# Four weight slots outside the ring, refilled through the whole expert loop: even experts read their first half there, odd experts in the ring

## The chip, the core and the metric

The kernel runs on one core of a Trainium2 chip, in float32. Its time is the device time of one execution in microseconds (us); the time of a version is the median of several executions. A profile is taken of one further execution. The engines are PE (TensorE), DVE (VectorE), ACT (ScalarE), POOL (GpSimd) and SP (SyncE), which here does nothing but issue transfers; 16 DMA engines move the data.

## The reference

One decoder layer for 256 prompt tokens and 8 sample tokens: a mixer (an RG-LRU group beside a convolution group), cross-attention, and then 32 routed experts of which each token takes four. The change lies in the experts:

```python
def run_block(args):
    e, idx = args
    xb = x_pad[idx]
    gu = xb @ w_e1[e] + b_e1[e]
    g, u = gu[:, :D_EXPERT], gu[:, D_EXPERT:]
    g = jnp.minimum(g, SWIGLU_LIMIT)
    u = jnp.clip(u, -SWIGLU_LIMIT, SWIGLU_LIMIT)
    h = (u + 1.0) * (g * jax.nn.sigmoid(SWIGLU_ALPHA * g))
    return h @ w_e2[e] + b_e2[e]
```

`w_e1[e]` is 1024 x 2048 and `w_e2[e]` 1024 x 1024, so an expert has 12 MB of weights (1 MB = 1024 KB here), and all 32 are read once.

## The kernel before

**Slots.** On chip, weights stand in slots of 128 partitions x 2048 floats, 1 MB each. `ring` has `RING` = 12 of them. In the expert loop slots 0 to 7 hold `w_e1` of an expert (the eight blocks of its contraction) and slots 8 to 11 hold `w_e2`. They are filled two at a time, 2 MB in one transfer, into the even slot and the next. Four more slots, called `head`, lie outside the ring in memory that the attention no longer needs (`mn`, `kT`, `wgate` with a piece of `mix`, and `xT`). They are filled once, ahead of the loop, with the first half of expert 0; the ring then holds the rest of expert 0 and, in its slots 0 to 3, already the first half of expert 1.

**What PE does for an expert.** `up_bias(b)` waits for the bias row (`b1_filled`) and opens the sums with it (L1453); it reads `b1q`, the one buffer for a bias. `up` then takes slots 0 to 7 in order (L1539) and frees each with an increment of `freed`. ACT and DVE make the activation out of the sums (L1103, L686, L1106, L1109), PE turns it (`turn_h`, L1548), and `down` takes slots 8 to 11 (L1558), each again freed. Experts go in pairs `q`. In the even expert 2q, PE adds up the pair before (`rounds`, L1501) between `up` and `down`. In the odd expert, PE gathers the next pair's tokens (L1510) after slot 3 and after slot 7. Expert 0 is an exception: its bias is already in, and it takes a ring slot and a head slot in turn.

**What SP does.** SP issues all the weight transfers in the order of its program, each after a wait on `freed` for the slots that it writes. All of its transfers go through one hardware queue, q1. `expert(e, b)` issues six loads of 2 MB; the load for slots s and s + 1 waits until the expert before has used slot s + 1. The bias of expert e is a transfer of 8 KB, four rows of 2 KB, and it is issued before expert e's six loads, as soon as PE has used the bias of e - 1:

```python
with sp.Fori(2, NE) as e:
    sp.wait_ge(S["b1_used"], e)
    bias(e)
    expert(e, e)
```

Below, "load e:s" is the load of slots s and s + 1 for expert e; it fetches 2 MB. The last loads of the kernel are 31:0, 31:2, ..., 31:10. After the loop come the last rounds (L1501, L1617), the final norm on DVE (L1138, L1169) and the stores.

Of the kernel before, what the change touches and what calls it, by code (L numbers as in the profile page):

```python
# [76 lines left out]
HEAD_SLOTS = W_SLOTS // 2  # L77
KC_SLOTS = 8
# [28 lines left out]
def fills_before(n):  # L107

    return n // RING + 1 - (1 if n % RING < HEADROOM else 0)


def build(nc, a, outs):
    ctx = ExitStack()
    with ctx:
# [10 lines left out]
        EXPERT_W = ATTENTION_W + D  # L125
        MIXW = max(MIXER_W, EXPERT_W)
        mix = sb("mix", [P, MIXW])
        xT = sb("xT", [P, KD, TOK])
# [4 lines left out]
        mn = sb("mn", [P, KD, NMEM])  # L133
        kT = sb("kT", [P, KD, NMEM])
        wgate = sb("wgate", [P, 2, LC, P])
# [60 lines left out]
        head_u = mix[:, ATTENTION_W:EXPERT_W]  # L196
# [7 lines left out]
        def table(*shape):  # L204
# [17 lines left out]
        head = [v[:, 0:SLOT].rearrange("p (g c) -> p g c", g=2) for v in  # L222
                (mn[:, :, :].rearrange("p k m -> p (k m)"), kT[:, :, :].rearrange("p k m -> p (k m)"),
                 xT[:, :, :].rearrange("p k t -> p (k t)"))]
        head = [(v[:, 0, :], v[:, 1, :]) for v in head]
        head.insert(2, (wgate[:, :, :, :].rearrange("p g c i -> p (g c i)"), head_u))
# [40 lines left out]
        head_filled consts zeroed ident_ready pick_ready freed kc_freed  # L267
# [45 lines left out]
        def _(sp):  # L313
# [50 lines left out]
            def fill_head(k):  # L364
                for gu in range(2):
                    sp.dma_start(head[k][gu], a["w_e1"][0, 0, DEAL[k], D * gu:D * gu + D]).then_inc(S["head_filled"], 16)


            sp.wait_ge(S["freed"], freed_after(KV_ENTRY[7]))
            fill_head(0)  # L370
            sp.wait_ge(S["score_done"], H)
            fill_head(1)
            fill_head(2)
# [8 lines left out]
            fill_head(3)  # L382
# [13 lines left out]
            with sp.If(n > 0):  # L396
                sp.wait_ge(S["table_ready"], 1)
                with sp.Fori(0, n) as j:
                    e = sp.value_load(tabi[0:1, 0, bass.ds(j, 1)], min_val=0, max_val=NE - 1)
                    sp.wait_ge(S["b1_used"], j + NE)  # L400
                    bias(e)
                    expert(e, j + NE)
# [771 lines left out]
        def _(pe):  # L1174
# [346 lines left out]
            def up(b, e2, between, outside=False):  # L1521

                if not outside:
                    up_bias(b)
                order = list(range(W_SLOTS))
                if outside:
                    order = [k for i in range(HEAD_SLOTS) for k in (HEAD_SLOTS + i, i)]
                for n_done, k in enumerate(order):
                    g_u = (ring[:, k, 0:D], ring[:, k, D:2 * D])
                    if outside and k < HEAD_SLOTS:  # L1530
                        pe.wait_ge(S["head_filled"], 2 * 16 * HEAD_SLOTS)
                        g_u = head[k]
                    elif k < HEAD_SLOTS:
                        pe.wait_ge(filled[k - k % 2], 16 * b + 16 * (fills_before(MOE0 + k) - 1))
                    else:
                        pe.wait_ge(filled[k - k % 2], 16 * b + 16 * fills_before(MOE0 + k))
                    for gu in range(2):
                        for i in range(2):
                            m = pe.matmul(ps[gu][CAP * i:CAP * i + CAP, :], xeT[:, k, CAP * e2:CAP * e2 + CAP],  # L1539
                                          g_u[gu][:, 512 * i:512 * i + 512],  # L1540
                                          start=False, stop=(n_done == W_SLOTS - 1))
                    m.then_inc(S["freed"], 1)
                    between(k)
# [20 lines left out]
            def pair(q, first):  # L1564
# [10 lines left out]
                if first:  # L1575
                    up(2 * q, 0, lambda k: None, True)
                    turn_h(2 * q)
                else:
                    up(2 * q, 0, lambda k: None)
# [6 lines left out]
                up(2 * q + 1, 1, gather_next)  # L1586
# [34 lines left out]
            with pe.If(n > 0):  # L1621
# [7 lines left out]
                with pe.Fori(0, n) as j:  # L1629
# [4 lines left out]
                    up(j + NE, 0, lambda k: None)  # L1634
# [34 lines left out]
```

## Time and profile before

| what | value |
|---|---|
| median of 3 executions | 1260.92 us (1260.77 to 1263.11) |
| the profiled execution's own time | 1263.79 us |
| its span, first to last instruction | 1261.4 us |
| PE busy | 1163.7 us (92%) |
| DMA queue q1, share of 16 engines | 87.5% |
| read from HBM | 453.71 MB |
| granted TensorE clock, mean | 0.980 of 2.4 GHz |

The profile cuts the span in 40 slices of 31.5 us. The expert loop lies between 312 us and 1247 us, slices 10 to 39. Matmuls overlap, so a busy PE is not one that could do no more; where PE waits for a transfer, the timeline has the wait in brackets behind the instruction that waited.

### The profile page before, as it was taken

What the parts mean: (1) busy time and instruction counts of PE and PEld (TensorE: products, weight loads), DVE (VectorE), ACT (ScalarE), POOL (GpSimd) and SP (SyncE); (2) the same over time, 40 slices, a digit from 0 to 9 for tenths busy, and PEclk for the clock granted to TensorE, in tenths of its full rate; (3) what the DMA queues carried; (4) which work ended last, traced back from release to release, by engine and by line L of the source; (5) the groups of instructions that cost most, each with busy time, mean ns of one, the idle gap of its engine ahead of it and who ended that gap; (6) DMA issues with size and microseconds to landing.
All of it is one profiled execution on the core that took longest, in us unless ns stands there. A gap on an engine that the chain in (4) does not pass through costs nothing.

```text
span 1261.4 us, 14407 instructions
## 1 busy us (share of the span) xinstructions
PE 1163.7 (92%) x5540; PEld 572.1 (45%) x5540; DVE 338.5 (27%) x820; ACT 182.1 (14%) x354; POOL 27.8 (2%) x54
## 2 busy tenths in 40 slices
PE   8999999698899999999998998989998989898996
PEld 6887888387333433434333333334333323232332
DVE  3795424515112121220212121212112021212123
ACT  3114213103010101011110101011110101010102
POOL 4000001100000000000000000000000000000000
PEclk9999999798889999999999999999999999999999
DMA  9398433993689999999999999999999999999993
GB/s 304 91 291 275 137 102 134 357 410 122 241 351 418 428 428 428 427 429 428 426 430 426 429 428 428 428 427 429 427 430 426 429 428 428 427 430 426 430 427 143
DMA packets 65381, 457.38 MB, mean 363 GB/s; under 512 B 4788, under 2 KB 33676, under 8 KB 41030
## 3 DMA queue, kind: packets, MB, share of 16 engines
q1 hardware_dynamic: 63408, 452.26, 87.5%
q10 hardware_dynamic: 1117, 3.04, 0.6%
q0 software_dynamic: 832, 1.76, 0.5%
q8 instruction: 16, 0.26, 0.1%
q14 instruction: 8, 0.06, 0.0%
HBM read 453.71 MB, written 3.81 MB: 363 GB/s over the span
## 4 chain that ended last, share of the span: by engine, by line
PE 56%; DMA 37%; DVE 4%; ACT 2%; issue 1%; ACTq 0%; POOL 0%; SPq 0%; DVEq 0%
DMA ring<-in_w_e 36%; PE ps L1539 21%; PE ps L1250 11%; PE ps L1558 8%; PE ps L1269 3%; PE ps L1501 3%; DVE ring L955 2%; PE ps L1510 2%; PE ps L1453 1%; PE ps L1412 1%; PE ps L1548 1%; PE ps L1499 1%; PE ps L1197 1%; PE ps L1186 1%; PE ps L1444 1%
## 5 line engine op out<-in xcount | busy, mean ns | idle before, releaser
L1539 PE MATMUL ps<-ring,mix 128*64 128x512 f32 x2016 | 452.2, 597 | 27.1 <-DMA ring<-in_w_e 25.0
L1539 PEld LDWEIGHTS ps<-ring,mix 128*64 128x64 f32 x2016 | 137.1, 137 | 326.6 <-issue 257.1
L1558 PE MATMUL ps<-ring,mix 128*64 128x512 f32 x1024 | 232.7, 607 | 22.0 <-issue 11.0
L1103 DVE TENSOR_SCALAR mix<-ps 128x512 f32<-128x512 f32 x32 | 22.1, 692 | 601.4 <-PE ps L1539 601.4
L1558 PEld LDWEIGHTS ps<-ring,mix 128*64 128x64 f32 x1024 | 78.7, 139 | 155.4 <-issue 141.2
L686 ACT ACTIVATE mix<-mix 128x512 f32<-128x512 f32 x32 | 20.2, 630 | 415.8 <-DVE mix L1103 415.8
L1510 PEld LDWEIGHTS ps<-mix 128*128 128x128 f32 x544 | 68.0, 200 | 14.4 <-issue 13.0
L1510 PE MATMUL ps<-mix 128*128 128x128 f32 x544 | 72.6, 288 | 1.3 <-ACT rstd L668 1.3
L696 ACT ACTIVATE mix<-ps 64x512 f32<-64x512 f32 x64 | 37.9, 592 | 226.5 <-PE ps L1558 226.1
L1090 DVE SCALAR_TENSOR_TENSOR mix<-mix,gates 128x1024 f32<-128x1024 f32 x16 | 20.5, 1284 | 151.5 <-ACT mix L696 151.5
L1501 PE MATMUL ps<-mix 128*128 128x512 f32 x128 | 59.2, 605 | 1.3 <-ACT mix L696 1.3
L1250 PE MATMUL ps<-mix,ring 128*128 128x264 f32 x256 | 58.8, 393 | 0.3 <-ACT mix L639 0.3
L1269 PE MATMUL ps<-ring,mn 128*128 128x256 f32 x256 | 56.1, 379 | 0.0
L1250 PEld LDWEIGHTS ps<-mix,ring 128*128 128x128 f32 x256 | 49.5, 194 | 9.1 <-ACT mix L639 0.4
L1269 PEld LDWEIGHTS ps<-ring,mn 128*128 128x128 f32 x256 | 48.6, 190 | 6.6
L1084 DVE TENSOR_TENSOR tok<-tok,ps 128x512 f32<-128x512 f32 (+1 forms) x70 | 43.5, 681 | 15.3 <-PE ps L1499 14.1
L841 DVE SCALAR_TENSOR_TENSOR mix<-mix,par 128x256 f32<-128x256 f32 x120 | 47.6, 491 | 0.0
L1250 PE MATMUL ps<-sq,ring 128*128 128x264 f32 x192 | 44.6, 396 | 0.0
L1250 PEld LDWEIGHTS ps<-sq,ring 128*128 128x128 f32 x192 | 37.4, 196 | 6.6
L1501 PEld LDWEIGHTS ps<-mix 128*128 128x128 f32 x128 | 23.0, 189 | 37.3 <-issue 35.1
L1250 PE MATMUL ps<-xn,ring 128*128 128x264 f32 x176 | 39.6, 387 | 0.0
L1548 PE MATMUL ps<-ident,mix 128*128 128x128 f32 x128 | 22.6, 300 | 15.4 <-DVE mix L1109 15.4
(294 smaller groups left out, 657.7 us busy)
## 6 DMA issues: line engine op xcount, KB each, us to landing
ring<-in_w_e SPq DMA_DIRECT2D x190, 2048.0 KB, 23.7
ring<-in_w_in SPq DMA_DIRECT2D x8, 1024.0 KB, 15.2
ring<-in_cache_mem_k SPq DMA_DIRECT2D x8, 1024.0 KB, 4.9
ring<-in_cache_mem_v SPq DMA_DIRECT2D x8, 1024.0 KB, 8.4
ring<-in_w_k SPq DMA_DIRECT2D x4, 1024.0 KB, 8.9
ring<-in_w_v SPq DMA_DIRECT2D x4, 1024.0 KB, 12.5
ring<-in_w_out SPq DMA_DIRECT2D x4, 1024.0 KB, 12.4
ring<-in_w_q SPq DMA_DIRECT2D x4, 1024.0 KB, 12.0
```

The source lines that it names most:

```text
L696: m = act.activation(ysb[CAP * e2:CAP * e2 + CAP, 512 * i:512 * i + 512], ps[3][CAP * i:CAP * i + CAP, :], ACT.Copy)
L841: dve.scalar_tensor_tensor(out=gc[:, c, 0:SEQ], in0=gpad[:, c, bass.ds(w, SEQ)], scalar=par[:, bass.ds(4 * w + (C_WCF + c), 1)], in1=gc[:, ...
L955: last = dve.tensor_tensor_reduce(key[:, t, h, :], key[:, t, h, :], q, 1.0, 0.0, ALU.mult, ALU.add, sT[:, t, 4 * b + h:4 * b + h + 1])
L1084: last = dve.tensor_tensor(dst, dst, ps[bank + i][0:rows, :], ALU.add)
L1103: dve.tensor_scalar(g1, ps[0][:, :], LIMIT, None, ALU.min).then_inc(S["g_clamped"], 1)
L1250: m = pe.matmul(ps[o % 4][:, 0:TOK], wslot(n)[:, k, half * P:(half + 1) * P], (xn if o < 4 else sq)[:, k, :] if kind == "in" else src(k), ...
L1269: m = pe.matmul(ps[KV_BANK[j]][:, 256 * t:256 * t + 256], mn[:, k, P * t:P * t + P], wslot(n)[:, k, :], start=(k == 0), stop=(k == KD - 1))
L1501: m = pe.matmul(ps[bank + i][:, :], gT[:, t0:t0 + P], ysb[:, cols], start=True, stop=True)
L1510: m = pe.matmul(ps[4 + i][:, P * (k % 4):P * (k % 4) + P], xnt[:, t, DEAL[k]], sel[:, t, :], start=(t == 0), stop=(t == 1))
L1539: m = pe.matmul(ps[gu][CAP * i:CAP * i + CAP, :], xeT[:, k, CAP * e2:CAP * e2 + CAP], g_u[gu][:, 512 * i:512 * i + 512], start=False, stop ...
L1548: m = pe.transpose(ps[2][:, j * P:(j + 1) * P], hh[:, j:4 * P:4], ident[:, :])
L1558: m = pe.matmul(ps[3][CAP * i:CAP * i + CAP, :], hTv[:, k % 4, CAP * (k // 4):CAP * (k // 4) + CAP], ring[:, s, D * (k % 2) + 512 * i:D * ...
```

## The change

Each head slot is from now on refilled during the loop. The two tensors `mixed` and `low` replace `mn`, `kT`, `mix`, `wgate` and `xT`, so that each pair of head slots is one piece of memory: `low` for slots 0 and 1, `high` (the end of `mixed`) for slots 2 and 3. A pair of them takes one transfer of 2 MB, with its own semaphore.

- Even experts read slots 0 to 3 from `low` and `high`; odd experts read them from the ring. So load e:0 or e:2 goes where expert e - 2 read its own. Slots 4 to 11 stay as they were.
- Ahead of the loop the same half of expert 0 is fetched; of slots 2 and 3 the part `LATE` = 1984 of 4096 columns comes early and the rest where `head[3]` came.
- Expert 0 takes its slots in the order 4, 5, 0, 1, 6, 7, 2, 3. During it, SP issues 1:4, 2:0, 1:6, 2:2, then 1:8 and 1:10.
- SP's loop is over pairs. The bias of expert e is issued behind load e:4.

```diff
+FIRST_ORDER = [4, 5, 0, 1, 6, 7, 2, 3]
...
-            def expert(e, b, first=0):
-
-                for s in range(first, RING, 2):
-                    fill(e, s, RING * b + freed_after(MOE0 + s + 1 - RING))
+            def refill(e, s, free):
+
+                sp.wait_ge(S["freed"], free)
+                sp.dma_start((low[:, :], high)[s // 2], first_weight(e, s)).then_inc(S[("low_filled", "high_filled")[s // 2]], 16)
+
+            def used(b, s):
+
+                return RING * b + freed_after(MOE0 + s)
+
+            def rest(e, b):
+
+                fill(e, 4, used(b - 1, 5))
+                sp.wait_ge(S["b1_used"], b)
+                bias(e)
+                fill(e, 6, used(b - 1, 7))
+                fill(e, 8, used(b - 1, 9))
+                fill(e, 10, used(b - 1, 11))
...
+            fill(1, 4, used(0, FIRST_ORDER.index(5)))
             sp.wait_ge(S["b1_used"], 1)
             bias(1)
-
-            for s in range(HEAD_SLOTS, W_SLOTS, 2):
-                fill(1, s, freed_after(MOE0 + 2 * (s + 1 - HEAD_SLOTS)))
-            expert(1, 1, W_SLOTS)
-            with sp.Fori(2, NE) as e:
-                sp.wait_ge(S["b1_used"], e)
-                bias(e)
-                expert(e, e)
+            refill(2, 0, used(0, FIRST_ORDER.index(1)))
+            fill(1, 6, used(0, FIRST_ORDER.index(7)))
+            refill(2, 2, used(0, FIRST_ORDER.index(3)))
+            fill(1, 8, used(0, 9))
+            fill(1, 10, used(0, 11))
+
+            def two_experts(q, last):
+
+                for s in range(0, HEAD_SLOTS, 2):
+                    fill(2 * q + 1, s, used(2 * q - 1, s + 1))
+                rest(2 * q, 2 * q)
+                if not last:
+                    for s in range(0, HEAD_SLOTS, 2):
+                        refill(2 * q + 2, s, used(2 * q, s + 1))
+                rest(2 * q + 1, 2 * q + 1)
+
+            with sp.Fori(1, PAIRS - 1) as q:
+                two_experts(q, False)
+            two_experts(PAIRS - 1, True)
...
-            def up(b, e2, between, outside=False):
+            def up(b, q, e2, between, even=False, outside=False):
...
-                for n_done, k in enumerate(order):
-                    g_u = (ring[:, k, 0:D], ring[:, k, D:2 * D])
-                    if outside and k < HEAD_SLOTS:
-                        pe.wait_ge(S["head_filled"], 2 * 16 * HEAD_SLOTS)
-                        g_u = head[k]
-                    elif k < HEAD_SLOTS:
-                        pe.wait_ge(filled[k - k % 2], 16 * b + 16 * (fills_before(MOE0 + k) - 1))
+                for n_done, k in enumerate(FIRST_ORDER if outside else range(W_SLOTS)):
+                    w = ring[:, k, :]
+                    if k >= HEAD_SLOTS:
+                        pe.wait_ge(filled[k - k % 2], 16 * b + 16 * fills_before(MOE0 + k))
+                    elif not even:
+                        pe.wait_ge(filled[k - k % 2], 16 * q + 16 * fills_before(MOE0 + k))
                     else:
-                        pe.wait_ge(filled[k - k % 2], 16 * b + 16 * fills_before(MOE0 + k))
+                        w = head[k]
+                        pe.wait_ge(S[("low_filled", "high_filled")[k // 2]], 16 * q + 32)
```

The first place is SP's loop. Before, one turn of it is one expert e: the bias first (`in_b_e1`), then the six loads, four from `w_e1` and two from `w_e2`. These are the turn's first rows, as far as its third load:

```order
L361 ISA [waits b1_used]
L361 DMA mix<-in_b_e1 4x512
L345 ISA
L353 ISA [waits freed]
L353 DMA ring<-in_w_e1 128x4096
L345 REGISTER_ALU
L353 ISA [waits freed]
L353 DMA ring<-in_w_e1 128x4096
L345 REGISTER_ALU
L353 ISA [waits freed]
L353 DMA ring<-in_w_e1 128x4096
```

After the change one turn is a pair. Its first two loads are (2q+1):0 and (2q+1):2, the next is 2q:4, and only then comes the bias of 2q:

```order
L356 ISA [waits freed]
L356 DMA ring<-in_w_e1 128x4096
L348 REGISTER_ALU
L356 ISA [waits freed]
L356 DMA ring<-in_w_e1 128x4096
L348 REGISTER_ALU
L356 ISA [waits freed]
L356 DMA ring<-in_w_e1 128x4096
L377 ISA [waits b1_used]
L377 DMA mixed<-in_b_e1 4x512
L348 REGISTER_ALU
L356 ISA [waits freed]
```

So the bias has moved from ahead of an expert's first load to behind the third load of the same stretch. In the middle of the turn the same piece comes again for the odd expert, with `low` and `mixed` as the targets of the two loads ahead:

```order
L361 ISA [waits freed]
L361 DMA low<-in_w_e1 128x4096
L360 REGISTER_ALU
L361 ISA [waits freed]
L361 DMA mixed<-in_w_e1 128x4096
L348 REGISTER_ALU
L356 ISA [waits freed]
L356 DMA ring<-in_w_e1 128x4096
L377 ISA [waits b1_used]
L377 DMA mixed<-in_b_e1 4x512
```

The second place is expert 0's stretch of SP's program, just ahead of the loop. Before, it is the bias of expert 1 and loads 1:4, 1:6, 1:8, 1:10:

```order
L361 DMA mix<-in_b_e1 4x512
L353 DMA ring<-in_w_e1 128x4096 x2
L353 DMA ring<-in_w_e2 128x4096 x2
```

After, it has two loads more, 2:0 into `low` and 2:2 into `mixed`:

```order
L356 DMA ring<-in_w_e1 128x4096 [waits freed]
L377 DMA mixed<-in_b_e1 4x512 [waits b1_used]
L361 DMA low<-in_w_e1 128x4096 [waits freed]
L356 DMA ring<-in_w_e1 128x4096 [waits freed]
L361 DMA mixed<-in_w_e1 128x4096 [waits freed]
L356 DMA ring<-in_w_e2 128x4096 [waits freed] x2
```

## Rows read from the trace of the kernel before

**Rows 1.** The page's 40 slices: PE, granted clock, DMA share and rate.

```profile
PE   8999999698899999999998998989998989898996
...
PEclk9999999798889999999999999999999999999999
DMA  9398433993689999999999999999999999999993
GB/s 304 91 291 275 137 102 134 357 410 122 241 351 418 428 428 428 427 429 428 426 430 426 429 428 428 428 427 429 427 430 426 429 428 428 427 430 426 430 427 143
```

**Rows 2.** Stretches of the loop: busy us of each engine, PEclk, DMA share, GB/s.

```profile
312.00:318.00 6.00, 5.79 (x28) 2.46 (x30) 0.00 (x0) 0.11 (x1) 0.00 (x0) 1.00 0.00 0
318.00:338.00 20.00, 16.32 (x65) 5.83 (x62) 4.22 (x12) 1.23 (x2) 0.00 (x0) 0.83 0.58 211
338.00:368.00 30.00, 29.30 (x136) 12.07 (x132) 4.98 (x8) 3.67 (x7) 0.00 (x0) 0.92 1.01 418
368.00:373.00 5.00, 5.00 (x20) 1.46 (x20) 0.26 (x1) 0.00 (x0) 0.00 (x0) 0.78 0.04 16
...
388.00:1240.00 852.00, 792.32 (x3790) 304.41 (x3787) 157.23 (x314) 89.36 (x162) 0.00 (x0) 1.00 1.00 427
```

**Rows 3.** The chain that ended last, expert 3 and experts 29 to 31: start, us, what.

```profile
405.21 7.02 PE ps L1539 x32
...
1147.03 25.66 DMA ring<-in_w_e
...
1172.74 3.68 PE ps L1539 x16
1176.43 0.04 SPq L353
...
1176.57 25.64 DMA ring<-in_w_e
...
1206.08 25.66 DMA ring<-in_w_e
1231.75 0.04 issue
1231.79 3.68 PE ps L1539 x16
```

**Rows 4.** PE's timeline, experts 30 and 31: start, us, instructions [wait before them].

```profile
1187.80 1.09 PE L1453 MATMUL ps<-mix,ones 1*64 1x512 f32 x8
1188.82 7.31 PE L1539 MATMUL ps<-ring,mix 128*64 128x512 f32 x32
1197.37 3.65 PE L1539 MATMUL ps<-ring,mix 128*64 128x512 f32 x16 [1.24 <-DMA ring<-in_w_e]
1202.25 3.65 PE L1539 MATMUL ps<-ring,mix 128*64 128x512 f32 x16 [1.23 <-DMA ring<-in_w_e]
...
1217.71 1.09 PE L1453 MATMUL ps<-mix,ones 1*64 1x512 f32 x8
1218.73 7.09 PE L1539 MATMUL ps<-ring,mix 128*64 128x512 f32 x32
...
1228.00 7.45 PE L1539 MATMUL ps<-ring,mix 128*64 128x512 f32 x32
```

**Rows 5.** PE's timeline: the start of expert 0, and the pair of experts 2 and 3.

```profile
312.21 1.94 PE L1539 MATMUL ps<-ring,mix 128*64 128x512 f32 x8 [1.11 <-issue]
...
377.35 1.09 PE L1453 MATMUL ps<-mix,ones 1*64 1x512 f32 x8
378.37 13.95 PE L1539 MATMUL ps<-ring,mix 128*64 128x512 f32 x64
...
404.13 1.09 PE L1453 MATMUL ps<-mix,ones 1*64 1x512 f32 x8
...
432.91 1.09 PE L1453 MATMUL ps<-mix,ones 1*64 1x512 f32 x8
```

**Rows 6.** SP's timeline: the issue of expert 31's bias.

```profile
1189.10 0.56 SPq L361 DMA_DIRECT2D mix<-in_b_e  x1
```

**Rows 7.** Two places where the granted clock fell in the loop: PE's timeline.

```profile
329.16 1.13 PE L1548 MATMUL ps<-ident,mix 128*128 128x128 f32 x4 [3.00 <-DVE mix L1109]
330.98 9.62 PE L1558 MATMUL ps<-ring,mix 128*64 128x512 f32 x32 [0.69 <-ACT mix L690]
...
885.49 8.78 PE L1558 MATMUL ps<-ring,mix 128*64 128x512 f32 x32 [0.73 <-issue]
...
1239.84 7.09 PE L1558 MATMUL ps<-ring,mix 128*64 128x512 f32 x32 [0.73 <-issue]
```

**Rows 8.** Stretches of 2 us in which the clock was at its lower level.

```profile
332.00:334.00 2.00, 2.00 (x8) 0.59 (x6) 0.00 (x0) 0.00 (x0) 0.00 (x0) 0.50 0.00 0
336.00:338.00 2.00, 2.00 (x12) 0.70 (x10) 0.00 (x0) 0.00 (x0) 0.00 (x0) 0.97 0.00 0
```

More of the change, by code:

```diff
@@ L124, in build @@
         ATTENTION_W = 2 * KD * TOK + 2 * H * 2 * NMEM + 2 * D + 4 * NB * H + 2 * P
[L125 to L128, printed above, removed]
+        MIXW = max(MIXER_W, ATTENTION_W)
+        LATE = 2 * SLOT - KD * TOK
+        low = sb("low", [P, 2 * SLOT])
+        mixed = sb("mixed", [P, MIXW + 2 * LC * P + KD * TOK])
+        mix = mixed[:, 0:MIXW]
+        wgate = mixed[:, MIXW:MIXW + 2 * LC * P].rearrange("p (g c i) -> p g c i", g=2, c=LC)
+        xT = mixed[:, MIXW + 2 * LC * P:MIXW + 2 * LC * P + KD * TOK].rearrange("p (k t) -> p k t", k=KD)
+        high = mixed[:, MIXW + 2 * LC * P + KD * TOK - 2 * SLOT:MIXW + 2 * LC * P + KD * TOK]
+        mn = low[:, 0:SLOT].rearrange("p (k m) -> p k m", k=KD)
+        kT = low[:, SLOT:2 * SLOT].rearrange("p (k m) -> p k m", k=KD)
         xn = sb("xn", [P, KD, TOK])
@@ L219, in build @@
         gateT = rstd[0:NE, :]
[L222 to L226, printed above, removed]
+        assert MIXW + 2 * LC * P + KD * TOK - 2 * SLOT >= ATTENTION_W
+        head = [v[:, SLOT * i:SLOT * i + SLOT] for v in (low, high) for i in range(2)]
         tabi = sb("tabi", [1, 2, P], I32)
@@ L341, in _, with first_weight @@
                             sp.dma_start(stage_b[r0:r0 + rows, :], src).then_inc(S["par_loaded"], 16)
+            def first_weight(e, s):
+                return a["w_e1"][0][bass.ds(e, 1), s * P:(s + 2) * P, :].rearrange("o (p t) c -> p (o t c)", t=2)
             def fill(e, s, free):
@@ L362, in bias @@
                     S["b1_filled"], 16)
-            def fill_head(k):
-                for gu in range(2):
-                    sp.dma_start(head[k][gu], a["w_e1"][0, 0, DEAL[k], D * gu:D * gu + D]).then_inc(S["head_filled"], 16)
             sp.wait_ge(S["freed"], freed_after(KV_ENTRY[7]))
-            fill_head(0)
+            sp.dma_start(low[:, 0:SLOT], a["w_e1"][0, 0, DEAL[0], :]).then_inc(S["low_filled"], 16)
             sp.wait_ge(S["score_done"], H)
-            fill_head(1)
-            fill_head(2)
+            sp.dma_start(low[:, SLOT:2 * SLOT], a["w_e1"][0, 0, DEAL[1], :]).then_inc(S["low_filled"], 16)
+            sp.dma_start(high[:, 0:LATE], first_weight(0, 2)[:, 0:LATE]).then_inc(S["high_filled"], 16)
             for s in range(HEAD_SLOTS, W_SLOTS, 2):
@@ L399, in _ @@
                     e = sp.value_load(tabi[0:1, 0, bass.ds(j, 1)], min_val=0, max_val=NE - 1)
-                    sp.wait_ge(S["b1_used"], j + NE)
-                    bias(e)
-                    expert(e, j + NE)
+                    for s in range(0, HEAD_SLOTS, 2):
+                        fill(e, s, used(j + NE - 1, s + 1))
+                    rest(e, j + NE)
             for t in range(2):
@@ L1575, in pair @@
                 if first:
[L1576 removed]
+                    up(2 * q, q, 0, lambda k: None, True, True)
                     turn_h(2 * q)
                 else:
[L1579 removed]
+                    up(2 * q, q, 0, lambda k: None, True)
                     pe.wait_ge(S["y_ready"], 2 * q)
@@ L1585, in pair @@
                 down(2 * q)
-                up(2 * q + 1, 1, gather_next)
+                up(2 * q + 1, q, 1, gather_next)
                 gather(q + 1, (1,))
```

17 lines of the change are left out of this document (5 added, 12 removed).

## The prediction

> **What bounds the kernel now.** I read the 40 slices first. From the fourteenth slice to the last but one the DMA row is full, at 426 to 430 GB/s [rows 1], and the stretch 388 to 1240 us taken as one has a share of 1.00 at 427 GB/s [rows 2]. Ahead of it the DMA engines have holes: nothing moves from 312 to 318 us, 211 GB/s from 318 to 338, and 16 GB/s from 368 to 373 [rows 2]. Those holes are SP waiting for a free slot.
>
> The chain says the same in another way. Near the end it is one load of 25.65 us, two slots of matmuls of 3.68 us, the next load [rows 3]. PE takes up the load's slots at 1172.74, then 29.5 us later, and last at 1231.79. In 29.5 us six loads of 2 MB land, so one takes 4.92 us. A load that lands 25.65 us after its issue has thus four others before it in the queue: slots come free long before they can be refilled, and the rate of the DMA engines sets the pace, not the number of slots.
>
> How far behind is PE? Early, with no wait, an even expert takes 404.13 - 377.35 = 26.78 us and an odd one 432.91 - 404.13 = 28.78 us [rows 5]. The loads allow 29.5 us each. So PE has 2.7 us to spare in an even expert and 0.7 us in an odd one.
>
> **What the change removes and adds. First term, the slots.** Holes can be filled only where a slot comes free earlier than before. That is so once: in expert 0, where the head slots used to lie idle after use. Two more loads, 2:0 and 2:2, are issued there, 2 x 4.92 = 9.8 us of transfer. From 318 to 338 us, 20 us at 211 GB/s moved 4.2 million bytes, which are two loads; four take 19.7 us. Expert 0 begins at 312.21, and two slots of matmuls take 3.5 us (eight take 13.95) [rows 5], so the first load can go out at 315.7 and the four are through by about 336, before the slots of `down` come free at 338. The hole holds them, and nothing behind is late.
>
> From then on, count the loads by the event that releases them. Before, the use of slot s + 1 of expert e - 1 releases load e:s, for all six s. After, for s of 4 and more it releases the same load e:s; for s of 0 and 2 it releases (e+1):s. At each event 2 MB, in both versions. So the queue is as long as before at each moment, the hole at 368 to 373 us stays, and **loads e:4 to e:10 land when they landed before**. Only the loads for slots 0 to 3 land earlier, by a whole expert. Were they late? PE sat at slots 4 and 6 of expert 30, 1.24 and 1.23 us, and its matmuls of slots 0 to 3 took 7.31 us where those of expert 31 took 7.09, 0.2 us [rows 4]; and that 0.2 is only taken out of the next wait. The lead of two loads is held as four full slots in memory and never spent, except in the last pair: there is no load 32:0 or 32:2, so 31:4 to 31:10 land 9.8 us earlier. But expert 31 had waited only 7.45 - 7.09 = 0.36 us for them [rows 4]; the rest of the 9.8 finds PE behind. First term: -0.4 us at the most.
>
> **Second term, the bias.** `up_bias` stands at the head of an expert, ahead of slots 0 to 3. Before, the bias of 31 is issued at 1189.10 and needed at 1217.71 [rows 4, 6]; it lies in the queue ahead of load 31:0. After, it lies behind 31:4, three loads later, and of expert 30 behind 30:4. When does that land? PE's slot 4 of expert 30 ended its wait at 1197.37 [rows 4], and by the count above 30:4 lands at that time again. The 8 KB behind it add about 0.1. So **expert 30 can't begin before 1197.5**, where it began at 1187.80 [rows 4]: 9.7 us late.
>
> What is given back? The waits of expert 30. Four slots take 7.02 us with no wait [rows 3], two 3.51. Slot 4 would have begun without a wait at 1188.82 + 7.02 = 1195.84 and did at 1197.37: 1.53. Slot 6 at 1197.37 + 3.51 = 1200.88 and did at 1202.25: 1.37. Both are gone, since their loads have landed by then: 2.9 us. In expert 31 the 0.36 goes as well, which is the first term. Expert 31 itself doesn't wait for its bias: 31:4 now lands four loads after 30:4, at 1197.4 + 19.7 = 1217.1, and PE comes at 1197.5 + 26.9 = 1224.4. What follows, to the end of the kernel, hangs on PE. The sum is 9.7 - 2.9 - 0.4 = **+6.4 us**. By the durations of an unhindered expert it is 1197.5 + 26.8 - 1217.71 - 0.36 = +6.2. I take +6.3.
>
> Does the DMA pace hold when PE is late? Slot 7 comes free 9.7 - 2.9 = 6.8 us later. The load then has 25.65 - 6.8 = 18.9 us from issue to landing, of which it needs 4.9 itself: three loads are still queued. So the loop keeps its 29.5 us per expert; what is lost is lost once, as a later place of PE against the loads, and only the end of the kernel pays it. PE's waits change their place: at the head of an odd expert 29.5 - 26.8 = 2.7 us, at the head of an even one 29.5 - 28.8 = 0.7 us. They begin some experts earlier than the first waits of before.
>
> **Third term, code and memory.** PE runs the same matmuls on the same shapes; a pair has one register instruction less or more here and there, which I take as 0. Ahead of the loop the same bytes are loaded. The load of slots 2 and 3 is split otherwise, 64 columns of 128 rows later: 32 KB, under 0.1 us, and expert 0 comes to slot 2 at about 322 us.
>
> **The time.** The sum is made against the profiled execution: 1263.79 + 6.3 = 1270.1. That one stands 2.9 us above the median of the runs, so the median becomes 1260.92 + 6.3 = 1267.2.
>
> **The rivals.**
>
> *The lead arrives (faster).* If the two loads of lead moved every landing, the loop would end 9.8 us earlier: 1251.1. For it speaks that the DMA row is the full one. Against it speaks the count: each load that PE waits for has two more ahead of it in the queue, the two of the lead. It would decide if PE had waited for slots 0 to 3, and those waits are 0.2 us. "Perfetto Trace Analysis", section Optimization Strategy, of the Trainium skill says that consistent bubbles can mean too little SBUF for the next tile; by that rule four more slots would close the 1.24 us bubbles here. The trace speaks against it, since the DMA share in the same stretch is 1.00. Chance 0.05.
>
> *The bias doesn't gate (no change).* If 8 KB passed the 2 MB loads, only -0.4 is left: 1260.5. Against it: the same queue, and loads that land 25.65 us after issue. Chance 0.04.
>
> *The bias lands early.* It has four rows, a load 128, so it need not use all DMA engines. If those that it uses run ahead of the others by up to a load, it lands up to 4.9 us earlier, expert 30 begins at 1192.6, and its slot 4 at 1200.6, still behind the load's 1197.4. Then the loss is 6.3 - 4.9 = 1.4 at the least: 1262.3 to 1266. "DMA: Bandwidth & Descriptors", section Queues, rings and completion order, says that descriptors are taken in ring order on each engine, but that completion isn't first in, first out over DMAs spread over different numbers of engines. No row here shows how far the engines lie apart. Chance 0.08.
>
> *The clock.* After a PE wait of 3.00 us the granted clock was 0.50, the 1.2 GHz level [rows 7, 8], and `down` took 9.62 us where it takes 7.09; a second fall, at 885 us, cost 8.78 - 7.09 = 1.7 [rows 7]. The new wait of 2.7 us at the head of each odd expert comes near that first one. The spare 3.4 us of a pair swallows it, except what is left at the head of expert 30: after a fall in expert 29 it begins 1.7 - 0.7 = 1.0 to 2.9 - 0.7 = 2.2 us later. Then 1268.2 to 1269.4. Chance 0.18.
>
> *Later still.* If the bias were done only with the load behind it, 4.9 more: 1272. Chance 0.04.
>
> The forecast itself has 0.61; its own range, from the two ways to work out the sum and the half us of a fall that is partly swallowed, is 1266 to 1268.
>
> **How the numbers follow.** A change within 0.2% is 2.5 us, about what a measurement of this kernel can tell from none: 1258.4 to 1263.4. The forecast, the clock and the later bias are slower, as is half or more of the early bias: 0.61 + 0.18 + 0.04 + 0.05 = 0.88. Within: 0.03 + 0.04 = 0.07. Faster: 0.05. The range 1264 to 1271 holds the forecast, the clock and part of the early bias, 0.61 + 0.18 + 0.04 = 0.83.
>
> **What would show it.** In the new profile: between 318 and 338 us over 400 GB/s; 368 to 373 us still empty; the share 1.00 after it. PE's waits for loads at the `up` matmuls nearly gone, and in their place waits ahead of the bias matmuls, some 2.7 and 0.7 us in turn. Expert 30's bias matmuls near 1197.5. The last load landing near 1232 instead of 1231.75 + 2 x 4.92 = 1241.6, with PE 6 us later than before. The prediction is wrong if the bias matmuls don't wait, if slots 4 and 6 still do, or if the landing of 30:4 has moved.

## The result, and the profile after

The changed kernel takes 1270.69 us, the median of five executions (1268.37 to 1273.34), beside 1260.94 us before (five executions, 1260.77 to 1263.42). The ratio is 1.0068, with a 95% interval of 1.0048 to 1.0088: slower, by 6 to 11 us. A later measurement of the same kernel gave 1.0047 (1.0035 to 1.0059). The profiled execution took 1270.69 us with a span of 1268.4; that of before 1263.79 with 1261.4. So the two traces differ by 6.9 us, where the medians differ by 9.75. The time ahead of the loop is part of that; it is taken up below, under "Where an execution starts its loop".

The page's 40 slices of the changed kernel, the lines that answer to [rows 1]:

```profile
PEclk9989999898889999999999999999999999999999
DMA  9398323993989999999999999999999999999970
GB/s 302 90 295 269 137 100 133 354 407 129 398 351 415 428 429 428 428 429 427 429 428 427 430 426 428 430 427 428 428 429 429 427 429 427 429 429 426 429 309 35
```

The eleventh slice went from 241 to 398 GB/s: the hole of expert 0 is filled. The last two slices went from 427 and 143 to 309 and 35: the loads are over earlier. The same in chosen stretches, the lines that answer to [rows 2], and behind them three from the end of the loop (clock, DMA share and GB/s are the last three figures):

```profile
312.00:318.00 6.00, 6.00 (x30) 2.42 (x28) 0.00 (x0) 0.00 (x0) 0.00 (x0) 1.00 0.31 66
318.00:338.00 20.00, 16.31 (x64) 5.81 (x62) 4.22 (x12) 1.23 (x2) 0.00 (x0) 0.83 1.00 412
338.00:368.00 30.00, 29.30 (x134) 11.88 (x130) 5.24 (x8) 3.67 (x7) 0.00 (x0) 0.92 0.97 412
368.00:373.00 5.00, 5.00 (x22) 1.62 (x20) 0.00 (x0) 0.00 (x0) 0.00 (x0) 0.81 0.16 36
...
1206.00:1232.00 26.00, 25.31 (x114) 8.71 (x112) 6.61 (x16) 2.41 (x4) 0.00 (x0) 1.00 0.86 341
...
1208.00:1210.00 2.00, 2.00 (x12) 0.60 (x10) 0.00 (x0) 0.00 (x0) 0.00 (x0) 1.00 0.31 131
...
1232.00:1242.00 10.00, 10.00 (x56) 4.49 (x52) 0.00 (x0) 0.38 (x1) 0.00 (x0) 1.00 0.12 49
```

The last of these stretches in the kernel before:

```profile
1232.00:1242.00 10.00, 8.44 (x46) 4.30 (x44) 2.67 (x4) 2.10 (x4) 0.00 (x0) 1.00 0.59 252
```

The two extra loads fit into 318 to 338 us, and the hole at 368 to 373 us is still there. In stretches of 2 us the last weights arrive by 1234 us, before the change by about 1240: some 6 us sooner, not the 9.8 us of two loads. The DMA engines have gaps in the last pair (a share of 0.31 from 1208 to 1210 us), where no load 32:0 or 32:2 stands in the queue and PE is late to free the slots. The kernel still ends 7 us later. What does PE wait for? First the view of PE's waits before (us in total, times, longest), then after:

```profile
PE ps L1539 <- DMA ring<-in_w_e: 25.0, 21, 1.3
```

```profile
PE ps L1478 <- DMA mixed<-in_b_e: 27.2, 17, 2.7
```

The 21 waits for weights are gone. In their place PE waits 17 times ahead of L1478, the bias matmuls, for the transfer of 8 KB, up to 2.7 us. PE's timeline of the changed kernel from expert 28's `down` to expert 31's first half, to be laid beside [rows 4]:

```profile
1159.09 7.09 PE L1580 MATMUL ps<-ring,mixed 128*64 128x512 f32 x32 [0.69 <-ACT mixed L715]
1167.80 1.26 PE L1478 MATMUL ps<-mixed,ones 1*64 1x512 f32 x8 [1.62 <-DMA mixed<-in_b_e]
1168.99 8.56 PE L1561 MATMUL ps<-ring,mixed 128*64 128x512 f32 x32
...
1198.23 1.09 PE L1478 MATMUL ps<-mixed,ones 1*64 1x512 f32 x8
1199.25 3.65 PE L1561 MATMUL ps<-low,mixed 128*64 128x512 f32 x16
1202.73 3.60 PE L1561 MATMUL ps<-mixed 128*64 128x512 f32 x16
1206.16 7.04 PE L1561 MATMUL ps<-ring,mixed 128*64 128x512 f32 x32
...
1225.00 1.09 PE L1478 MATMUL ps<-mixed,ones 1*64 1x512 f32 x8
```

Expert 30 begins at 1198.23, where it began at 1187.80: 10.4 us late. Its slots 0 to 7 go through without a wait, which gives back 3.1 us, and expert 31 begins at 1225.00 where it began at 1217.71: 7.3 us late. From there to the end it is 43.4 us (43.7 before). Expert 29 shows a cost that the sum didn't have: its matmuls of slots 0 to 3 took 8.56 us instead of 7.09, behind a wait of 1.62 us. The clock had fallen, as the stretches there show (the third figure from the right is the granted clock):

```profile
1168.00:1170.00 2.00, 2.00 (x12) 0.40 (x7) 0.00 (x0) 0.00 (x0) 0.00 (x0) 0.65 0.94 401
1170.00:1172.00 2.00, 2.00 (x8) 0.61 (x6) 0.00 (x0) 0.00 (x0) 0.00 (x0) 0.50 1.02 434
```

In stretches of 2 us from 372 to 1240 us, the changed kernel has eight such falls, the kernel before one (at 885 us, [rows 7]). Only the one in expert 29 can reach the end: the earlier ones are followed by further waits for a bias, which take them up.

The chain that ended last has changed in kind. Before, a load was its link of 25.65 us [rows 3]; after, it is the bias:

```profile
1080.43 10.48 PE ps L1561 x48
...
1090.92 0.04 SPq L356
...
1091.57 17.24 DMA mixed<-in_b_e
...
1108.86 1.09 PE ps L1478 x8
```

Slots 4 and 5 are used, SP issues the load for them and the bias behind it, and the next expert begins when that bias lands.

**Where an execution starts its loop.** Executions differ ahead of the loop, whatever the kernel. In the eleven profiles of this document expert 2 begins near 374 us (373.94 to 374.23, four of them) or between 375.96 and 377.82 us (the other seven, the kernel before and both profiles of the changed kernel among them). The difference is the granted clock in experts 0 and 1. PE's timeline of the changed kernel, and then of a kernel of the other kind (`a5` below), with `down` of expert 0 and the start of expert 2; in between, in expert 1, one group of L1524 takes 3.60 us in the first and 1.98 in the second:

```profile
330.47 9.68 PE L1580 MATMUL ps<-ring,mixed 128*64 128x512 f32 x32 [0.69 <-ACT mixed L715]
...
376.91 1.09 PE L1478 MATMUL ps<-mixed,ones 1*64 1x512 f32 x8
```

```profile
330.38 8.46 PE L1580 MATMUL ps<-ring,mixed 128*64 128x512 f32 x32 [0.69 <-ACT mixed L715]
...
373.94 1.09 PE L1478 MATMUL ps<-mixed,ones 1*64 1x512 f32 x8
```

So traces are best compared from the start of expert 2 to the end of the span. In the kernel before that is 1261.4 - 377.35 = 884.1 us; the others are given against it:

| profile | expert 2 begins | end of span | from there to the end | against before | forecast, without falls |
|---|---|---|---|---|---|
| changed kernel | 376.91 | 1268.4 | 891.5 | +7.4 | +6.3 |
| changed kernel, second profile (c1) | 377.82 | 1271.2 | 893.4 | +9.3 | +6.3 |
| bias first (a1) | 374.05 | 1257.5 | 883.5 | -0.6 | -0.4 |
| bias one load earlier (a2) | 376.47 | 1261.7 | 885.2 | +1.2 | +1.3 |
| bias one load later (a3) | 377.62 | 1298.4 | 920.8 | +36.7 | +11.2 |
| before, bias late (b1) | 374.23 | 1267.6 | 893.4 | +9.3 | +8.9 |
| matmuls in the wait (a4) | 376.10 | 1268.3 | 892.2 | +8.2 | +6.3 |
| the same, not in the last pair (a5) | 373.94 | 1264.7 | 890.8 | +6.7 | +6 |
| rotating slots (s1) | 375.96 | 1249.9 | 873.9 | -10.1 | -9.8 |
| rotating, one bias buffer (s2) | 373.94 | 1253.4 | 879.5 | -4.6 | -5.7 |

### The profile page after: what moved, and what is told of

Same layout as the page of the kernel before. It is cut to its first block, busy times and chain, and to the rows that moved or that the text cites. A ratio compares the mean times of both kernels' runs of the same rounds, so it can differ in the third digit from the quotient of the medians.

```text
span 1268.4 us, 14301 instructions
## 1 busy us (share of the span) xinstructions
PE 1169.2 (92%) x5540; PEld 579.3 (46%) x5540; DVE 338.4 (27%) x820; ACT 182.1 (14%) x354; POOL 28.3 (2%) x54
## 4 chain that ended last, share of the span: by engine, by line
PE 68%; DMA 22%; DVE 5%; ACT 2%; issue 1%; SPq 1%; ACTq 0%; POOL 0%; DVEq 0%
PE ps L1561 32%; DMA mixed<-in_b_e 22%; PE ps L1275 11%; PE ps L1580 9%; PE ps L1294 3%; PE ps L1535 3%; PE ps L1478 3%; DVE ring L980 2%; PE ps L1526 1%; PE ps L1570 1%; DVE mixed L1131 1%; DVE mixed L1128 1%; DVE mixed L1134 1%; PE ps L1524 1%; PE ps L1222 1%
## 5 line engine op out<-in xcount | busy, mean ns | idle before, releaser
L1561 PE MATMUL ps<-ring,mixed 128*64 128x512 f32 x1536 | 354.0, 615 | 1.1 <-issue 1.1
L1580 PE MATMUL ps<-ring,mixed 128*64 128x512 f32 x1024 | 231.1, 604 | 22.0 <-issue 11.0
L1561 PEld LDWEIGHTS ps<-ring,mixed 128*64 128x64 f32 x1536 | 111.0, 141 | 228.1 <-issue 226.2
L1580 PEld LDWEIGHTS ps<-ring,mixed 128*64 128x64 f32 x1024 | 78.2, 139 | 154.3 <-issue 140.1
L1535 PEld LDWEIGHTS ps<-mixed 128*128 128x128 f32 x544 | 68.1, 200 | 14.4 <-issue 13.0
L1535 PE MATMUL ps<-mixed 128*128 128x128 f32 x544 | 72.7, 288 | 1.3 <-ACT rstd L693 1.3
L1478 PE MATMUL ps<-mixed,ones 1*64 1x512 f32 x256 | 35.5, 624 | 27.2 <-DMA mixed<-in_b_e 27.2
L1526 PE MATMUL ps<-mixed 128*128 128x512 f32 x128 | 59.2, 605 | 1.3 <-ACT mixed L721 1.3
L1275 PE MATMUL ps<-mixed,ring 128*128 128x264 f32 x256 | 58.9, 393 | 0.3 <-ACT mixed L664 0.3
L1561 PE MATMUL ps<-low,mixed 128*64 128x512 f32 x256 | 58.4, 598 | 0.0
L1561 PE MATMUL ps<-mixed 128*64 128x512 f32 x256 | 57.7, 592 | 0.0
L1294 PE MATMUL ps<-ring,low 128*128 128x256 f32 x256 | 56.1, 379 | 0.0
L1275 PEld LDWEIGHTS ps<-mixed,ring 128*128 128x128 f32 x256 | 49.6, 194 | 9.1 <-ACT mixed L664 0.4
## 6 DMA issues: line engine op xcount, KB each, us to landing
ring<-in_w_v SPq DMA_DIRECT2D x4, 1024.0 KB, 11.2
```

Of the source, the lines that this page charges most:

```text
L1275: m = pe.matmul(ps[o % 4][:, 0:TOK], wslot(n)[:, k, half * P:(half + 1) * P], (xn if o < 4 else sq)[:, k, :] if kind == "in" else src(k), ...
L1294: m = pe.matmul(ps[KV_BANK[j]][:, 256 * t:256 * t + 256], mn[:, k, P * t:P * t + P], wslot(n)[:, k, :], start=(k == 0), stop=(k == KD - 1))
L1478: m = pe.matmul(ps[gu][CAP * i:CAP * i + CAP, :], ones[r:r + 1, 0:CAP], b1q[r:r + 1, :], start=True, stop=False)
L1526: m = pe.matmul(ps[bank + i][:, :], gT[:, t0:t0 + P], ysb[:, cols], start=True, stop=True)
L1535: m = pe.matmul(ps[4 + i][:, P * (k % 4):P * (k % 4) + P], xnt[:, t, DEAL[k]], sel[:, t, :], start=(t == 0), stop=(t == 1))
L1580: m = pe.matmul(ps[3][CAP * i:CAP * i + CAP, :], hTv[:, k % 4, CAP * (k // 4):CAP * (k // 4) + CAP], ring[:, s, D * (k % 2) + 512 * i:D * ...
```

## Experiments

My theory, Q: the whole loss is the bias's place in the queue, since an expert can't begin before its bias, and the bias now lies behind a load that is needed later than it. The rivals: S, the refilled slots cost by themselves; L, the lead of two loads is worth something once the bias is out of the way; C, beside Q, falls of the clock add to it. Each kernel was timed against the kernel before on the same chip.

### The bias issued first again

```diff
             def two_experts(q, last):
 
+                next_bias(2 * q, 2 * q)
                 for s in range(0, HEAD_SLOTS, 2):
                     fill(2 * q + 1, s, used(2 * q - 1, s + 1))
                 rest(2 * q, 2 * q)
+                next_bias(2 * q + 1, 2 * q + 1)
...
-                sp.wait_ge(S["b1_used"], b)
-                bias(e)
```

> The changed kernel, with the bias of each expert issued where the kernel before issues it: ahead of the six loads of its stretch, so ahead of loads (e+1):0, (e+1):2 and e:4. Theory Q (the bias's place in the queue is the whole loss): the bias lands 14.7 us earlier, no expert waits for it, and only the last pair's 0.4 us is left of the change: 1260.5 us, and the granted clock in the loop as before. Rival S (the refilled slots themselves cost, or PE reads them more slowly): it stays at 1268 to 1271. Rival L (the lead of two loads is worth something once the bias is out of the way): up to 9.8 us under before, 1251.

Measured: 1260.97 us (11 executions), ratio 0.9996 (0.9986 to 1.0006). The loss is gone, nothing is gained, and the profile has no fall of the clock in the loop. Rival S falls with it, for this kernel refills the same slots by the same loads. Rival L falls too in this form: the lead is there, the stretch 318 to 338 us ran at 417 GB/s, and it brings nothing. PE waits for weights as before, at slots 4 and 6 of expert 30 (PE's timeline):

```profile
1193.80 3.65 PE L1567 MATMUL ps<-ring,mixed 128*64 128x512 f32 x16 [1.41 <-DMA ring<-in_w_e]
1198.69 3.65 PE L1567 MATMUL ps<-ring,mixed 128*64 128x512 f32 x16 [1.24 <-DMA ring<-in_w_e]
```

That is the 1.24 and 1.23 us of [rows 4], with 0.2 us moved from slot 2 to slot 4, as the count of the loads by their events has it.

### One load earlier, one load later

```diff
             def rest(e, b):
 
-                fill(e, 4, used(b - 1, 5))
                 sp.wait_ge(S["b1_used"], b)
                 bias(e)
+                fill(e, 4, used(b - 1, 5))
```

> The changed kernel, with the bias just ahead of load e:4 instead of just behind it: one load, 4.9 us, earlier in the queue. Theory Q: expert 30 begins at 1192.6 instead of 1197.5, its waits of 2.9 us are gone, and the end is 1192.6 + 26.8 - 1217.7 - 0.4 = +1.3 us against before: 1262.2 us, a little more where the clock falls. PE's wait for the bias stays in the timeline at 2.7 and 0.7 us. Rival S: 1268 to 1271, as with the bias behind.

Measured: 1263.81 us (12 executions), ratio 1.0014 (1.0003 to 1.0025), +1.8 us. As Q has it. The bias waits stand in the timeline, and the pace of the loads is untouched; the three experts 29, 30 and 31:

```profile
1162.07 1.09 PE L1478 MATMUL ps<-mixed,ones 1*64 1x512 f32 x8 [2.65 <-DMA mixed<-in_b_e]
1191.58 1.09 PE L1478 MATMUL ps<-mixed,ones 1*64 1x512 f32 x8 [0.67 <-DMA mixed<-in_b_e]
1218.36 1.09 PE L1478 MATMUL ps<-mixed,ones 1*64 1x512 f32 x8
```

2.65 and 0.67 us are the 2.7 and 0.7 of the forecast, the same as in the changed kernel. The waits have their size from PE's spare time, whatever the place of the bias; what the place sets is how late PE runs against the loads. That can be read directly: expert 29, which waits for its bias in all of them, begins 790.9 us after expert 2 in the changed kernel and 785.6 us after it here (1162.07 - 376.47), 5.3 us sooner for one load of 4.92.

The other way, the bias behind `fill(e, 6, ...)`:

```diff
                 fill(e, 4, used(b - 1, 5))
+                fill(e, 6, used(b - 1, 7))
                 sp.wait_ge(S["b1_used"], b)
                 bias(e)
-                fill(e, 6, used(b - 1, 7))
```

> The changed kernel, with the bias behind load e:6: one load later. Theory Q: expert 30 begins at 1202.4, so +4.9 against the change: +11.2 against before without falls of the clock, 1272.2, and 1274 to 1276 with the 2 to 3 us that the changed kernel has above its sum. Rival S: no change against the changed kernel, 1268 to 1271.

Measured: 1296.04 us (5 executions), ratio 1.0275 (1.0254 to 1.0296), **+35 us where Q said +11**. The direction is Q's, the size is not, so something else begins here. Two odd experts, one pair apart, begin at a distance of 61.4 us (PE's timeline), where a pair took 59.05 before (1158.66 to 1217.71):

```profile
1134.73 1.66 PE L1478 MATMUL ps<-mixed,ones 1*64 1x512 f32 x8 [2.13 <-DMA mixed<-in_b_e]
1136.32 9.86 PE L1561 MATMUL ps<-ring,mixed 128*64 128x512 f32 x32
...
1196.11 1.60 PE L1478 MATMUL ps<-mixed,ones 1*64 1x512 f32 x8 [2.42 <-DMA mixed<-in_b_e]
```

And the DMA engines, full elsewhere, have two holes in that pair (stretches of 2 us; clock, DMA share and GB/s are the last three):

```profile
1138.00:1140.00 2.00, 2.00 (x8) 0.68 (x6) 0.00 (x0) 0.00 (x0) 0.00 (x0) 0.50 0.98 418
...
1142.00:1144.00 2.00, 2.00 (x12) 0.69 (x10) 0.00 (x0) 0.00 (x0) 0.00 (x0) 1.00 0.73 311
1144.00:1146.00 2.00, 2.00 (x12) 0.43 (x8) 0.00 (x0) 0.00 (x0) 0.00 (x0) 1.00 0.93 246
...
1164.00:1166.00 2.00, 2.00 (x12) 0.83 (x10) 0.00 (x0) 0.00 (x0) 0.00 (x0) 1.00 0.85 242
```

PE has become so late that slots come free after the queue has run out. At the start of the odd expert its `up` takes 9.86 us at the lower clock where 7.09 is usual, so its slots 4 to 7, and the bias behind them, go out 2.8 us later still. Thirteen falls stand in the loop, up to 7 us long, and gaps like these in most of its pairs. The loss then comes by the pair: from the start of expert 3 at 406.06 us to that of expert 29 at 1196.11 us thirteen pairs take 790.1 us, where 13 x 59.05 is 767.7. Those 22.4 us, 0 to 3.2 in a pair, are most of the 24 that are above Q's 11, and the loads never make them up. So a late bias costs once as long as the queue stays filled, and in each turn as soon as it doesn't.

### The kernel before, with only the bias late

```diff
             def expert(e, b, first=0):
 
                 for s in range(first, RING, 2):
                     fill(e, s, RING * b + freed_after(MOE0 + s + 1 - RING))
+                    if s == 4:
+                        sp.wait_ge(S["b1_used"], b)
+                        bias(e)
```

> The kernel before, with nothing changed but the place of the bias: behind load e:4 of its own six loads. Its head slots stay unused in the loop. Theory Q: expert 30 begins at 1197.5 as in the changed kernel, but 31:4 lands 9.8 us later than there, at 1226.8, and the bias of 31 behind it, so expert 31 begins at 1227.0 where it began at 1217.7: +9.3 - 0.4 = +8.9 us, 1269.8 us, more with falls of the clock. So the bias alone gives the loss, and the four slots take some of it back in the last pair. Rival S: the loss comes with the slots, and this kernel is at 1261.

Measured: 1272.07 us (5 executions), ratio 1.0089 (1.0073 to 1.0105). The bias alone makes the loss, without any refilled slot, and a little more of it. In its timeline expert 31 has the wait that the changed kernel doesn't have:

```profile
1165.14 1.09 PE L1452 MATMUL ps<-mix,ones 1*64 1x512 f32 x8 [1.75 <-DMA mix<-in_b_e]
...
1224.20 1.09 PE L1452 MATMUL ps<-mix,ones 1*64 1x512 f32 x8 [1.74 <-DMA mix<-in_b_e]
```

This is where the four slots do pay: by the count, 31:4 and the bias behind it land 9.8 us sooner in the changed kernel, and there expert 31 doesn't wait. Expert 31 begins 850.0 us after expert 2 here, where 1227.0 - 377.35 = 849.7 was forecast. The intervals of the two kernels overlap, so the 2.6 us between the two forecasts are shown by the timelines rather than by the times: +9.3 us here, where expert 31's wait takes up the fall in expert 29, against +7.4 and +9.3 in the changed kernel, of which 0.8 and 2.5 are that fall (below).

### Work in the wait, against the clock

```diff
                 down(2 * q)
+                if not first:
+                    for i in range(4):
+                        pe.matmul(ps[2][CAP * (i % 2):CAP * (i % 2) + CAP, :], ones[:, 0:CAP], xnt[:, 0, 0:512], start=True, stop=True)
                 up(2 * q + 1, q, 1, gather_next)
```

> The changed kernel, with four extra matmuls of 64x512 (1.8 us, their output is overwritten and used by nothing) ahead of the bias wait of each odd expert from 3 on. The bias stays where the change has it. Theory C (the 2 to 3 us that the changed kernel has above the sum of +6.3 are falls of the clock after its 2.7 us waits): the wait shrinks to some 0.9 us, the falls in the loop, eight in the changed kernel's profile, go to none or one, and the time is before + 6.3 us, a ratio of 1.0050 where the changed kernel had 1.0068. Rival N (the falls are swallowed by the spare time and the rest has another cause): falls gone, time as before them, 1.0068. If the extra matmuls cost by themselves in the early pairs, up to 1 us more.

Measured: 1270.48 us (6 executions), ratio 1.006 (1.0046 to 1.0074). The time alone decides nothing, by a slip of mine: in the last pair expert 31 has no wait, so there the extra matmuls cost their 1.8 us, which I hadn't counted. The profile fits theory C with this cost: two falls in the loop, none in expert 29, and +8.2 us from the start of expert 2, where 6.3 + 1.8 is 8.1. Hence once more, with `pair(PAIRS - 1, False)` taken out of the loop and free of them:

> The same four extra matmuls ahead of the bias wait of an odd expert, but not in the last pair, where expert 31 has no wait that could hide them and they cost their 1.8 us. Theory C (falls of the clock are what the changed kernel has above the sum): 1.8 us less than with them in all pairs, before + 6 us, a ratio of 1.0046 to 1.0050, and below the changed kernel, which runs beside it. Rival N: as the changed kernel.

> The changed kernel itself once more, as the neighbour on the same chip. Both theories: a ratio of about 1.0068 to before, 1268 to 1272 us, eight or so falls of the clock in the loop.

Measured: 1267.48 us (5 executions, 1267.07 to 1268.76), ratio 1.0039 (1.0026 to 1.0052), beside 1268.65 us (6 executions, 1267.41 to 1273.48), ratio 1.0047 (1.0035 to 1.0059), of the changed kernel. The medians are 1.2 us apart and the intervals overlap, so the times alone don't settle C. The traces say more. From one expert's late start to the next one's, 29 to 30, the three profiles have (PE's timeline) first the changed kernel in its second profile:

```profile
1168.96 1.55 PE L1478 MATMUL ps<-mixed,ones 1*64 1x512 f32 x8 [1.74 <-DMA mixed<-in_b_e]
1170.45 9.96 PE L1561 MATMUL ps<-ring,mixed 128*64 128x512 f32 x32
...
1201.09 1.09 PE L1478 MATMUL ps<-mixed,ones 1*64 1x512 f32 x8
```

and then the one with extra matmuls (L1610) in the wait:

```profile
1162.98 1.89 PE L1610 MATMUL ps<-mixed,ones 128*64 128x512 f32 x8
1164.91 1.09 PE L1478 MATMUL ps<-mixed,ones 1*64 1x512 f32 x8
1165.93 7.09 PE L1561 MATMUL ps<-ring,mixed 128*64 128x512 f32 x32
...
1194.52 1.09 PE L1478 MATMUL ps<-mixed,ones 1*64 1x512 f32 x8 [0.76 <-DMA mixed<-in_b_e]
```

Without a fall it is 1194.52 - 1164.91 = 29.6 us, the pace of the loads, with 0.76 us to spare. With a fall in expert 29 it is 1201.09 - 1168.96 = 32.1 us here and 1198.23 - 1167.80 = 30.4 us in the first profile. So a fall at this place adds 2.5 or 0.8 us that nothing takes up. It is all that sets the three loops apart: from the start of expert 2 they stand at +9.3, +7.4 and +6.7 us, and without their falls at 6.8, 6.6 and 6.7. Up to expert 29 there is no difference, which begins 791.0 us after expert 2 with the matmuls and 790.9 and 791.1 us after it without. Falls in the loop are three with the matmuls, eight in either profile without.

The whole times are less clear. The profiled execution with the longer fall took 1273.48 us, the longest of its six and 6.4 us more than the profiled one with the matmuls, but 3.9 of these stand already at the start of expert 2. The six executions spread by 6.1 us and those with the matmuls by 1.7, but the eleven of the kernel before, timed beside them, spread by 3.6. That a fall adds up to 2.5 us at the end of the loop is shown; how much falls add on average is an estimate of 1 to 2 us, from the ratios (1.0 us) and the means (1.9 us), with the part ahead of the loop in both.

### The lead put where it is needed

If a lead of two loads is worth nothing because only slots 0 to 3 have it, then slots 4 to 11 must have it too. All eight pairs of slots go into one rotation, load n where load n - 8 was, issued in the order of need; four experts make three rotations. Leaving only the core:

```diff
+        PHYS = ["low", "high", 4, 6, 8, 10, 0, 2]
+        BIAS = [b1q, b1r]
...
+            def step(j, m, last=False):
+
+                x, i = m // 6, m % 6
+                e = 4 * j + x
+                if i == 2:
+                    if not (last and x == 3):
+                        sp.wait_ge(S["b1_used"], e)
+                        bias(e + 1, (x + 1) % 2)
+                load(e, i, m % 8, used(4 * j + (m - 8) // 6, 2 * ((m - 8) % 6) + 1))
...
+            with sp.Fori(1, NE // 4 - 1) as j:
+                for m in range(24):
+                    step(j, m)
```

> All eight pairs of slots in one rotation: load n goes where load n - 8 was, for w_e1 and w_e2 alike, so loads are issued strictly in the order in which they are needed, as before the change, and the loop runs over four experts. Expert 0 takes its slots in order 0 to 7. The bias has two buffers and is issued one expert ahead. Theory L (a lead of two loads is worth its whole 9.8 us if the loads for slots 4 to 11 get it too, because the loop is bound by the rate of the loads and PE waits some 36 us in all): 31:6 lands 9.8 us earlier, the time is before - 9.8, a ratio of 0.992. Rival H (a hole elsewhere or PE takes the place): less than half of it, 0.996 or more.

Measured: 1251.41 us (6 executions), ratio **0.9913 (0.9899 to 0.9926)**, some 11 us under the kernel before and faster than both. The rate of the loads is the same 428 GB/s; they only reach PE earlier. PE's waits for weights have shrunk from 25.0 us to:

```profile
PE ps L1574 <- DMA ring<-in_w_e: 14.5, 12, 1.3
```

and experts 30 and 31 come sooner at the same pace, still waiting for a moment at slots 4 and 6 (PE's timeline):

```profile
1176.53 1.09 PE L1487 MATMUL ps<-mixed,ones 1*64 1x512 f32 x8
...
1190.85 3.65 PE L1574 MATMUL ps<-ring,mixed 128*64 128x512 f32 x16 [1.24 <-DMA ring<-in_w_e]
...
1206.31 1.09 PE L1487 MATMUL ps<-mixed,ones 1*64 1x512 f32 x8
```

Slot 6 of expert 30 is taken up at 1190.85, where it was 1202.25 before [rows 4]: 11.4 us sooner, the 9.8 us of the two loads and 1.6 us, of which 1.4 are the earlier start of expert 2 in this execution (375.96 where the kernel before had 377.35).

The same rotation with one bias buffer, `BIAS = [b1q, b1q]`, and so `bias(e)` in the place of `bias(e + 1, ...)`:

> The same rotation with one bias buffer, so that the bias of e can't be issued before expert e - 1 has used its own, which is just ahead of load e:4 in the queue. Theory Q: expert 31 begins when its bias lands, behind load 31:2, 9.8 us ahead of 31:6, and needs 13.9 us from there to slot 6, so it comes 4.1 us behind the load. The time is 4.1 us above the kernel with two buffers: before - 5.7, a ratio of 0.9955, a little more with falls of the clock. Rival: the bias has no effect in this order, both at 0.992.

Measured: 1258.14 us (6 executions), ratio 0.9963 (0.995 to 0.9977), 6.3 us above the kernel with two buffers by the means of the ratios. Q said 4.1 and more with falls; expert 31 has one:

```profile
1208.30 1.09 PE L1484 MATMUL ps<-mixed,ones 1*64 1x512 f32 x8 [2.72 <-DMA mixed<-in_b_e]
1209.32 8.78 PE L1571 MATMUL ps<-ring,mixed 128*64 128x512 f32 x32
```

Its 1.7 us are in the price: from the start of expert 2 the two kernels are 5.5 us apart, 3.8 without the fall, where Q said 4.1. So in this order too, where the bias stands ahead of the load that PE needs at slot 4, it costs more than half of what the lead brings.

## Why the prediction was right, and where it was off

**The slots bring nothing.** Right, and shown by two kernels from two sides: the change with the bias in its old place is at 0.9996, and the same memory used in one rotation is at 0.9913. The count of loads by the event that releases them was the step that carried this: it said that loads e:4 to e:10 keep their landings. The waits at slots 4 and 6 in the first experiment, 1.41 and 1.24 us, are those landings. The last loads of the kernel came some 6 us earlier rather than 9.8, which changed nothing, since PE was later still.

**The bias gates.** Right. Expert 30 was to begin at 1197.5 and began at 1198.23; given back were 3.1 us for 2.9; the waits ahead of odd and even experts were to be 2.7 and 0.7 us and were 2.65 and 0.67 where the clock didn't fall between them. Moving the bias by one load earlier moved the time as forecast, and moving it alone in the kernel before gave the whole loss.

**The size, where it was off.** The forecast was +6.3 us, the medians say +9.75, the ratio +8.6 (6 to 11), and the second measurement +5.9 (4.4 to 7.5). Two steps were off. The first is the clock. A fall in expert 29 was a rival with a chance of 0.18, and it happened in both profiles of the changed kernel, with eight falls in the loop of each, where the kernel before had one. Its price was to be 1.0 to 2.2 us; the two profiles give 0.8 and 2.5, one below and one above. The upper end rested on a fall of 2.9 us, for which the rows give 9.62 - 7.09 = 2.5. The forecast should have had the fall as the likely case: a wait of 2.7 us each pair comes close to the 3.00 us of [rows 7], and in the changed kernel's first profile seven of the eleven waits of 1.6 us or more had a fall behind them, in the second eight of eleven, where the forecast had one in five.

The second step is the last one, from the profiled execution to the median. For the profiled execution the sum gave 1270.1 us, and it took 1270.69. The 2.9 us between before's profiled execution and its median were then taken off. But that profiled execution was one that started its loop late, and the changed kernel's profiled execution, which also is its median, was another. Before's five executions lie at 1260.8 to 1260.9 (three) and 1263.1 to 1263.4 (two). That the lower ones start the loop some 3 us earlier is likely from the other kernels' profiles, but none of them was profiled, so it isn't shown. The changed kernel's median thus lies above the forecast's own 1266 to 1268, and inside the wide range, up to 1271, by 0.3 us; which kind of execution became the median decided that, and it was luck. The mechanism doesn't depend on it.

**The rules weighed against the forecast.** One was "DMA: Bandwidth & Descriptors" of the Trainium skill, section Queues, rings and completion order, by which transfers on different numbers of engines may complete out of turn. That would have shown as an earlier landing. The size of the waits can't tell, since it is PE's spare time wherever the bias stands; the place can. With the extra matmuls in the wait, where no fall is in the way, expert 30 waited for its bias and began 820.6 us after expert 2 (1194.52 - 373.94), where the forecast had 1197.5 - 377.35 = 820.2. So here the bias wasn't early. The rival that the lead arrives, with the rule on consistent bubbles of "Perfetto Trace Analysis", section Optimization Strategy, of the Trainium skill, fell for this change and not for the rotation: there more buffers did shorten the time, though the bubbles of 1.24 us stayed as they were.

**The pace holds.** Right for this change, 426 to 430 GB/s in the slices of the loop, but with less margin than the prediction made one believe. It had three loads still queued, and yet in the last pair, where two loads fewer are issued, gaps appeared at 1206 to 1212 us and again at 1220 to 1224; with the bias one load later the queue ran out in most pairs.

## What to carry to other kernels

Where loads set the pace, count for each freed slot which load it releases: a deeper buffer helps only if the loads that are waited for come forward, and slots given to those that were never late hold their lead unspent. A small transfer that opens a stage belongs ahead of the large ones that the stage needs later, and if its buffer forbids that, a second buffer of a few KB can be worth more than 4 MB of slots (6.3 us here, where the slots without it brought 4.7). What delays the consumer costs once while the queue is full, and in every turn once it runs empty; so ask how many loads are still queued when a slot comes free.

## What the runs showed of the hardware

TensorE's granted clock fell to 0.50, 1.2 GHz, after waits that are short. In each of the two profiles of the changed kernel there were eight falls in the loop: fifteen of the sixteen came after a wait of 1.6 to 2.7 us between dense matmuls and one after a wait of 0.96 us, each wait followed by 1.1 us or more of bias matmuls that use one row. Not each such wait was followed by a fall: the first profile had eleven waits of 1.6 us or more and seven falls behind them. The waits for weights in the kernel before, up to 1.3 us and with no bias matmuls behind them, went by with one fall in the loop, and those of up to 1.41 us in the kernel with the bias first with none. Extra matmuls, 1.9 us of them in each wait of an odd expert, brought the eight falls down to two in one profile and three in another. A fall showed as 8.56 or 9.96 us for 32 matmuls of 64x512 that take 7.09, and as 0.8 or 2.5 us at the end of the kernel.

A transfer of 8 KB, issued behind loads of 2 MB in the same hardware queue, landed 14.8 to 17.2 us after its issue, and 5.3 us sooner when it stood one load of 4.92 us earlier.
